# A gated attention trunk on one core: half of the memory's keys computed first, its norm applied after the product

## The reference

```
def rms_norm(x, g):
    y = x * rsqrt(mean(x * x, axis=-1, keepdims=True) + EPS)
    return y * g
...
memn = rms_norm(mem, norm_mem[l])           # 256 x 1024
h = h + cross_attention(hn, memn, w_xq[l], w_xkv[l], w_xo[l])
...
def cross_attention(hn, memn, wq, wkv, wo):
    q = (hn @ wq).reshape(B, S, X_HEADS, X_HD)
    k, v = jnp.split(memn @ wkv, 2, axis=-1)
    logits = einsum('bqhd,bkhd->bhqk', q, k) * (X_HD ** -0.5)
    p = softmax(logits)
    return einsum('bhqk,bkhd->bqhd', p, v).reshape(B, S, D_MODEL) @ wo
```

## Time and profile before

| | |
|---|---|
| median of 3 runs | 958.43 us (957.01 to 958.47) |
| profiled execution | 958.45 us |
| its span on the core | 956.7 us |
| TensorE, matmuls busy | 938.0 us |
| VectorE busy | 551.8 us |
| ScalarE busy | 408.9 us |
| GpSimd busy | 14.6 us |
| HBM read, written | 89.76 MB, 2.10 MB |
| DMA, mean | 97 GB/s |
| mean granted TensorE clock | 0.997 |

### The profile page before, as it was taken

The page is one execution under the profiler, slowest core; times in us unless marked ns, Lnnn a source line. Parts: engine busy times, 40 slices in busy tenths (PEclk is TensorE's granted clock), DMA queues, the critical chain, the costliest instruction groups (busy, mean ns, idle before and its releaser), DMA issues.

```text
span 956.7 us, 11786 instructions
## 1 busy us (share of the span) xinstructions
PE 938.0 (98%) x4605; PEld 762.0 (80%) x4605; DVE 551.8 (58%) x979; ACT 408.9 (43%) x676; POOL 14.6 (2%) x38
## 2 busy tenths in 40 slices
PE   7999999999998999999999999999999999999997
PEld 6878777777776878889988668888888888888885
DVE  6532676342547662778333534858947876885544
ACT  4431466444423323344434533455445545634522
POOL 4000000000000000000000000000000000000000
PEclk9999999999999999999999999999999999999999
DMA  8311221122112162442521242120441261063202
GB/s 288 128 42 53 89 88 45 45 88 88 48 41 89 45 228 83 140 143 77 211 88 36 97 175 78 55 89 1 151 158 45 87 221 45 1 202 107 88 1 88
DMA packets 44815, 92.62 MB, mean 97 GB/s; under 512 B 1772, under 2 KB 1864, under 8 KB 44760
## 3 DMA queue, kind: packets, MB, share of 16 engines
q1 hardware_dynamic: 43192, 86.54, 27.0%
q0 software_dynamic: 1568, 5.32, 1.7%
HBM read 89.76 MB, written 2.10 MB: 96 GB/s over the span
## 4 chain that ended last, share of the span: by engine, by line
PE 92%; DVE 4%; ACT 2%; issue 1%; DMA 1%; SPq 0%; ACTq 0%; DVEq 0%
PE bank L1341 68%; PE bank L1372 12%; PE bank L1545 1%; DVE w_lo L978 1%; PE bank L1439 1%; PE bank L1466 1%; PE bank L1451 1%; PE bank L1385 1%; PE bank L1496 1%; PE bank L1483 1%; PE bank L1523 1%; DMA stage<-in_w_in 1%; PE bank L1510 1%; ACT w_hi L727 1%; PE bank L1484 0%
## 5 line engine op out<-in xcount | busy, mean ns | idle before, releaser
L978 DVE TENSOR_TENSOR w_lo<-stage,w_hi 128x1024 fp32r<-128x1024 f32 x174 | 205.1, 1220 | 88.4 <-ACT w_hi L727 88.3
L1341 PE MATMUL bank<-act_hi,w_hi 128*128 128x512 f32 (+2 forms) x624 | 246.2, 394 | 1.1 <-DVE act_lo L1166 1.1
L1341 PE MATMUL bank<-act_hi,w_lo 128*128 128x512 f32 (+2 forms) x624 | 241.3, 387 | 0.0
L1341 PE MATMUL bank<-act_lo,w_hi 128*128 128x512 f32 (+2 forms) x624 | 240.8, 386 | 0.0
L727 ACT ACTIVATE w_hi<-stage 128x1024 fp32r<-128x1024 f32 x174 | 174.5, 1051 | 97.2 <-PE bank L1341 36.6
L1341 PEld LDWEIGHTS bank<-act_hi,w_hi 128*128 128x128 f32 x624 | 117.9, 189 | 23.4 <-issue 1.3
L1341 PEld LDWEIGHTS bank<-act_hi,w_lo 128*128 128x128 f32 x624 | 117.5, 188 | 23.9
L1341 PEld LDWEIGHTS bank<-act_lo,w_hi 128*128 128x128 f32 x624 | 117.8, 189 | 22.1
L1341 PE MATMUL bank<-w_hi,act_hi 128*128 128x512 f32 x256 | 101.6, 397 | 4.0 <-DVE act_lo L1166 2.6
L1341 PE MATMUL bank<-w_hi,act_lo 128*128 128x512 f32 x256 | 99.8, 390 | 0.0
L1341 PE MATMUL bank<-w_lo,act_hi 128*128 128x512 f32 x256 | 99.7, 390 | 0.0
(11 more groups left out here) (260 smaller groups left out, 1264.7 us busy)
## 6 DMA issues: line engine op xcount, KB each, us to landing
stage<-in_w_in SPq DMA_DIRECT2D x20, 1024.0 KB, 5.0
stage<-in_w_mlp_in SPq DMA_DIRECT2D x16, 1024.0 KB, 5.2
stage<-in_w_mlp_out SPq DMA_DIRECT2D x16, 1024.0 KB, 5.5
stage<-in_w_xkv SPq DMA_DIRECT2D x8, 1024.0 KB, 5.0
stage<-in_w_mix_out SPq DMA_DIRECT2D x4, 1024.0 KB, 4.9
stage<-in_w_xq SPq DMA_DIRECT2D x4, 1024.0 KB, 5.2
stage<-in_w_xo SPq DMA_DIRECT2D x4, 1024.0 KB, 5.0
x_tok<-in_x SPq DMA_DIRECT2D x4, 512.0 KB, 9.7
```

Source lines behind the costliest of these rows:

```text
L978: dve.tensor_tensor(w_lo[:, r:r + 2, :], stage_pair(pair), w_hi[:, r:r + 2, :].bitcast(F32), ALU.subtract).then_inc(s_low, 1)
L1341: ins = pe.matmul(dst, still[q], moving[q], start=(k == 0 and q == 0), stop=(k == nk - 1 and q == 2))
```

## The change

The unit mem_k0 is moved from after mix1 to the very front, ahead of fox_v, and is computed in another loop order: step k does all four groups with slab k, 12 matmuls of 256 columns, into banks 6 and 7 (`mem_products`). Its input is mem times the gains, without the roots: mem is loaded in two column halves, transposed (`mem_turn`), and split with the gain as a factor of the copy (`mem_split`), 256 columns at a time. The roots come later: squares on ScalarE, `mem_root` on VectorE, two diagonal tiles whose product with ones gives the factor of every memory row in all partitions (`mem_factors`), and the keys are multiplied by it as they leave PSUM (`mem_keys`, VectorE). The other half of the keys, mem_k1, stays in its place and is now taken out by VectorE with that factor instead of ScalarE's copy; the values get the root as the scale of their copy on ScalarE.

The split mem and the first keys are needed again after mix1, but their memory is not free in between. GpSimd writes them to DRAM (1 MB, 1 MB and 0.5 MB) and reads them back after the last merge_split. The zero padding of `conv_u` is written after those copies; ScalarE's conv and gate_rows steps and VectorE's fox_q wait for it (`s_pad`).

At the start the warm-up is 12 products (24 instructions), the load order is mem, gains, slab 0, slab 1, mem's other half, slabs 2-3, slabs 4-5, x tile 0, slabs 6-7, the row of norm_mix, fox_v's first lot, x tile 1, fox_v's second lot, x tiles 2 and 3. The norm steps of x are moved as the list shows: norm_turn of tiles 2 and 3 now stand after the second half of the group before, not after its first half.

```diff
-WARM_UP = 20
+WARM_UP = 12
...
     u = [
+        ("mem_k0", "w_xkv", 0, KT, 0, 4),
         ("fox_v", "w_in", 0, KT, C_FV, NT),
...
-        ("mem_k0", "w_xkv", 0, KT, 0, 4),
         ("mem_k1", "w_xkv", 0, KT, HALF_W, 4),
...
-    steps += [("norm", 0), ("split_weights", 0), ("norm_turn", 0), ("norm_split", 0), ("split_weights", 1),
-              ("norm", 1), ("split_weights", 2), ("norm_root", 1), ("split_weights", 3), ("norm_scale", 1)]
-    after(1, ("norm_turn", 1), ("norm_split", 1), ("norm", 2))
-    after(2, ("norm_turn", 2), ("norm_split", 2), ("norm", 3))
-    after(4, ("norm_turn", 3), ("norm_split", 3), ("split_weights", 4), ("split_weights", 5))
+    steps += [("mem_gains", 0), ("mem_turn", 0), ("mem_split", 0), ("split_weights", 0), ("mem_split", 1),
+              ("mem_turn", 1), ("mem_split", 2), ("mem_split", 3)]
+    after(0, ("split_weights", 1), ("mem_turn", 2), ("mem_split", 4), ("mem_split", 5))
+    after(1, ("split_weights", 2), ("mem_turn", 3), ("mem_split", 6), ("mem_split", 7))
+    after(2, ("split_weights", 3), ("norm", 0))
+    before(3, ("mem_squares", 0), ("mem_squares", 1))
+    after(3, ("split_weights", 4), ("split_weights", 5))
+    before(7, ("norm_turn", 0), ("norm_split", 0), ("norm", 1))
+    after(7, ("norm_root", 1), ("norm_scale", 1))
+    after(first("fox_v"), ("mem_root", 0))
+    after(first("fox_v") + 1, ("norm_turn", 1), ("norm_split", 1), ("norm", 2))
+    after(first("fox_v") + 2, ("mem_factors", 0), ("mem_keys", 0))
+    after(first("fox_v") + 3, ("norm_turn", 2), ("norm_split", 2), ("norm", 3))
+    after(first("fox_v") + 5, ("norm_turn", 3), ("norm_split", 3))
...
-    h = first("mix0")
-    for i in range(MEM // P):
-        after(h + 2 * i + 2, ("norm", NT + i))
-        after(h + 2 * i + 4, ("norm_turn", NT + i), ("norm_split", NT + i))
...
-        pairs.setdefault(f if early else max(f, min(f + 1, need - 2)), []).append(pair)
+        at_half = f if early else max(f, min(f + 1, need - 2))
+        pairs.setdefault(max(at_half, FIRST_HALF[1] - 1), []).append(pair)
...
+            pool.wait_ge(s_memhigh, KT)
+            pool.dma_start(kept_hi, mem_hi[:].bitcast(F32)).then_inc(s_kept, 16)
+            pool.wait_ge(s_memlow, KT)
+            pool.dma_start(kept_lo, mem_lo[:].bitcast(F32)).then_inc(s_kept, 16)
+            pool.wait_ge(s_memkeys, 4)
+            pool.dma_start(kept_k, mem_k[:, 0:4, :]).then_inc(s_kept, 16)
+            pool.wait_ge(s_kept, 16 * 3)
+            pool.memset(conv_u[:, :, 0:CONV_K - 1], 0.0).then_inc(s_pad, 1)
...
-            load_row(row_a, norm_mem, s_row_a)
-
-            pool.wait_ge(s_scaled, 2 * (NT + 2))
+            pool.wait_ge(s_merl, KT)
             load_row(row_b, norm_xattn, s_row_b)
+            pool.dma_start(mem_hi[:].bitcast(F32), kept_hi).then_inc(s_back, 16)
+            pool.dma_start(mem_lo[:].bitcast(F32), kept_lo).then_inc(s_back, 16)
+            pool.dma_start(mem_k[:, 0:4, :], kept_k).then_inc(s_back, 16)
...
-                elif k == "mem_k":
-                    copy(mem_k[:, 4 * order(n) + j, :], b[:, 0:MEM]).then_inc(free, 1)
...
-                    copy(mem_v[:, j, HALF_W * order(n):HALF_W * (order(n) + 1)], b[:]).then_inc(free, 1)
+                    copy(mem_v[:, j, HALF_W * order(n):HALF_W * (order(n) + 1)], b[:], scale=mem_stat[:, 2, j:j + 1])\
+                        .then_inc(free, 1)
...
+                elif step == "mem_split":
+                    act.wait_ge(s_memturn, n // 2 + 1)
+                    if n == 0:
+                        act.wait_ge(s_gain, 1)
+                    copy(mem_hi[:, n, :], mem_turned(n), scale=mem_gain[:, n:n + 1]).then_inc(s_memhigh, 1)
...
+                elif k == "mem_k":
+                    group_done(dve, g)
+                    dve.tensor_tensor(mem_k[:, 4 + j, :], b[:, 0:MEM], mem_factor[:], ALU.mult).then_inc(free, 1)
...
+                elif step == "mem_root":
+                    dve.wait_ge(s_memsquares, MEM // P)
+                    half_mean_square(mem_stat[:, 1, :], mem_stat[:, 0, :], DM)
+                    inverse_root(mem_stat[:, 2, :], mem_stat[:, 1, :], mem_stat[:, 3, :])
+                    for i in range(MEM // P):
+                        dve.tensor_scalar(mem_diag[:, i, :], ident[:], mem_stat[:, 2, i:i + 1], None, ALU.mult)\
+                           .then_inc(s_memdiag, 1)
+                elif step == "mem_keys":
+                    dve.wait_ge(s_half, KT)
+                    dve.wait_ge(s_memfactor, 1)
+                    for j in range(4):
+                        dve.tensor_tensor(mem_k[:, j, :], mem_product(j), mem_factor[:], ALU.mult).then_inc(s_memkeys, 1)
...
+            def mem_products(k):
+
+                pe.wait_ge(s_memlow, k + 1)
+                if k == 0:
+                    pe.wait_ge(s_slablow, 1)
+                elif k % 2 == 0 or k == 1:
+                    pe.wait_ge(s_low, k // 2 + 1)
+                for j in range(4):
+                    cols = slice(P * j, P * j + P)
+                    for q, (s, a) in enumerate(((w_hi, mem_hi), (w_hi, mem_lo), (w_lo, mem_hi))):
+                        ins = pe.matmul(mem_product(j), s[:, k, cols], a[:, k, :], start=(k == 0 and q == 0 and j % 2 == 0),
+                                        stop=(k == KT - 1 and q == 2 and j % 2 == 1))
+                ins.then_inc(s_half, 1)
```

More of the change, by code:

```diff
@@ L99 @@
 SLAB0 = [sum(u[3] for u in UNITS[:n]) for n in range(len(UNITS) + 1)]
-GROUP0 = [sum(u[5] for u in UNITS[:n] if u[3] <= KT) for n in range(len(UNITS) + 1)]
+GROUP0 = [sum(u[5] for u in UNITS[1:n] if u[3] <= KT) for n in range(len(UNITS) + 1)]
 def make_halves():
@@ L120, in make_halves @@
             groups = groups[2:]
+        if n == 0:
+            halves += [(n, j, c, 0, MEM) for c in cs for j in groups]
+            continue
         width = MEM if u[0].startswith("mem_k") else TOK
@@ L275, in make_steps @@
         after(first("up_ml1") + m - 4, ("merge_split", m))
-    h = first("mix0")
-    for i in range(MEM // P):
-        after(h + 2 * i + 2, ("norm", NT + i))
-        after(h + 2 * i + 4, ("norm_turn", NT + i), ("norm_split", NT + i))
-    for unit, n0, last in (("mix1", NT + 2, 5), ("x_out1", 2 * NT + 2, 3)):
+    for unit, n0, last in (("mix1", NT, 5), ("x_out1", 2 * NT, 3)):
         n = UNIT[unit]
@@ L657, in _ @@
             fill(pool.memset(ident[:], 0.0))
+            pool.wait_ge(s_const, n)
+            fill(pool.affine_select(out=ident[:], in_=ident[:], compare_op=ALU.not_equal, fill=1.0, base=0,
+                                    pattern=[[-1, P]], channel_multiplier=1))
+            assert n == N_IDENT
             fill(pool.memset(ident_b[:], 0.0))
@@ L664, in _ @@
             fill(pool.memset(decay[:].bitcast(F32), 0.0))
-            fill(pool.memset(conv_u[:], 0.0))
             fill(pool.memset(enter[:], 0.0))
@@ L668, in _ @@
             pool.wait_ge(s_const, n)
[L669 to L671 removed]
+            fill(pool.affine_select(out=ident_b[:], in_=ident_b[:], compare_op=ALU.not_equal, fill=1.0, base=0,
+                                    pattern=[[-1, P]], channel_multiplier=1))
             fill(pool.affine_select(out=hide_b[:], in_=hide_b[:], compare_op=ALU.is_ge, fill=HIDE, base=0,
@@ L1311, in source_ready @@
                 elif k % 4 == 0:
-                    tiles = {"mem_k": NT + 2, "mem_v": NT + 2, "x_q": 2 * NT + 2, "mlp_in": n_norm}.get(name, NT)
+                    if name in ("mem_k", "mem_v"):
+                        pe.wait_ge(s_back, 16 * 3)
+                        return
+                    tiles = {"x_q": 2 * NT, "mlp_in": n_norm}.get(name, NT)
                     if name == "mlp_in" and end < TOK:
@@ L1343, in half, with mem_turn @@
                 ins.then_inc(s_half, 1)
+            def mem_products(k):
[10 more added lines that the diff above has]
+                ins.then_inc(s_half, 1)
+            def mem_turn(b):
+                if b == 0:
+                    pe.wait_ge(s_const, N_IDENT)
+                pe.wait_ge(s_mem[b // 2], 16)
+                if b >= 2:
+                    pe.wait_ge(s_memlow, 2 * (b - 1))
+                for k in (2 * b, 2 * b + 1):
+                    for i in range(MEM // P):
+                        ins = pe.transpose(mem_turned(k)[:, P * i:P * i + P], mem_tok[:, i, P * k:P * k + P], ident[:])
+                ins.then_inc(s_memturn, 1)
             def product(i):
@@ L1555, in _ @@
                 if step == "half":
-                    product(n) if in_products(HALVES[n][0]) else half(n)
+                    if HALVES[n][0] == 0:
+                        mem_products(n)
+                    elif in_products(HALVES[n][0]):
+                        product(n)
+                    else:
+                        half(n)
+                elif step == "mem_gains":
+                    pe.wait_ge(s_const, N_IDENT)
+                    pe.wait_ge(s_gains, 16)
+                    pe.transpose(bank[1][:, 0:KT], gain_rows[:], ident[0:KT, 0:KT]).then_inc(s_gainturn, 1)
```

(8 more changed lines are left out.)

160 lines of the change are left out of this document (103 added, 57 removed).

## The result

The changed kernel took 975.14 us (median, 972.66 to 975.26) beside 958.45 for the kernel before (957.01 to 958.69): a ratio of 1.0172, interval 1.0157 to 1.0186. The forecast was 967, slower. The sign came, with nearly twice the size: +16.7 us where +9.0 stood in the sum, outside the range of 960.5 to 971.5. Its profiled execution took 975.26, its span 973.1.

The account below looks back on a forecast made before the run. The prediction took TensorE, busy 938.0 of 956.7 us, to bound the kernel. Start +4.8, clock +1.7 and middle +2.5 summed to +9.0 on 958.45, so 967 us, range 960.5 to 971.5.

Parts of the forecast that it names:

- the yardstick: At the start: fox_v has to end before 52.8 us, or the start has lost time.
- VectorE's queue: At the start: work ahead of tile 1's act_lo delays it to 34.1, so TensorE waits 5.4 us.
- the middle: At mem_k1: its copy, moved to VectorE behind two w_lo, makes TensorE wait 2.5 us (2.1 to 2.8).
- The floor: At the start: without the copies' delay fox_v ends at 54.6, +1.8 us; with loads that cost nothing 53.5, +0.7.
- the clock: Behind the wait for tile 1: granted clock falls to half, adding 1.7 us (0 to 3.4).
- the walk: Step-by-step timing of the start along the queues: fox_v ends at 54.6 before the copies to DRAM are added.
- Rival 2: At the start: 3.8 us earlier products are kept if tile 1's act_lo precedes 29 us; 957.3 or 954.8; 9%.
- the term for the loads: At the start: copies to DRAM delay later loads by up to 5.2 us; fox_v's end moves from +1.8 to +4.8.
- The start: Up to fox_v's end: +4.8 us taken, between ends of +1.8 and +7.1.
- Rival 3: At the start: too little warm-up, clock doesn't rise, memory unit at twice the pitch, fox_v ends at 63.4; 973; 8%.
- Rival 1: At the start: copies stay out of the loads' way and the clock holds; 961.7 to 962.8; 20%.
- Rival 4: After the start: waits for DRAM or the pad memset reach TensorE; 3% together with other ways.

Follow-up runs that it names:

- both late: Changed kernel with the copies to DRAM and the six small-element loads issued only after tile 1's lo part: 967.38 us, ratio 1.0105.
- the best kernel: Changed kernel with copies and small loads late, VectorE's mem_root, factors and fox_q splits later, tiles 2-3 turned earlier, x_q0's first splits later: 956.16 us, 0.9978.

## Why the prediction was right and wrong

**Right: the yardstick and VectorE's queue.** The 52.8 us at which fox_v has to end is the point where the time turns: 52.9 with VectorE's order mended, whose only other loss is the 2.3 us of the middle, gave 961.8; 50.0 gave 956.2. The order of VectorE's work was read right from the step lists, and its prices were right: tile 1's group at 34.58 for 34.1 once the loads were away, mem_root 2.2 us in both. The floor was too low all the same. Without either load fox_v ended 4.9 us behind the yardstick, 1.6 of it the clock, so 3.2 where the walk had 1.8 (and +0.7 for loads that cost nothing).

Rival 2 had the right lever and too much hope. It asked for tile 1's act_lo before 29 us, by pairs 8 and 9 and mem_root put later, and gave 957.3, or 954.8 with the middle mended. Those two moves, with the loads late, brought it to 30.71 and the time to 961.8. Only with tiles 2 and 3 turned earlier and the middle mended as well, and that act_lo at 29.82, did the kernel take 956.2.

**Right: the middle.** 2.3 us for 2.5 taken, by exactly the chain that was named: copy behind the two w_lo. VectorE and TensorE of the changed kernel:

```profile
475.10 2.35 DVE L1044 TENSOR_TENSOR w_lo<-stage,w_hi 128x1024 fp32r<-128x1024 f32 x2
...
477.37 0.75 DVE L1155 TENSOR_TENSOR mem_k<-bank,mem_factor 128x256 f32<-128x256 f32 x2
```
```profile
477.84 0.39 PE L1431 MATMUL bank<-mem_hi,w_hi 128*128 128x256 f32 x1 [2.27 <-DVE mem_k L1155]
```

**Wrong: the term for the loads.** The start was taken at +4.8, of which 3.0 were the loads (5.3 at full contention), and the clock was put at 1.7 beside it: +6.5. 13.0 came. The loads are 8.1 of it, the difference between the changed kernel (65.8) and the one with both late (57.65), at the same 1.6 of clock in each. The rest is the 3.2 above. Three steps failed.

1. Slabs 6-7 were put at 12.4, ahead of the sag. They are split at 14.1 with both loads late, and at 18.10 in the changed kernel: now they lie in the sag, which is as long as before (175 GB/s from 13 to 17 us, 189 in the kernel before). In the best kernel the small loads cost 3.9 us.
2. Copies were priced as a delay by their own bytes, 5.2 us, of which half was taken. From 20 to 25 us they held 75% of the engines, and q1 fell to 0.53 MB, where it moves 1.95 MB with the copies late. The lot that was in flight paid nearly all of it. The Trainium skill's page "DMA: Bandwidth & Descriptors", section "Queues, rings and completion order", which was cited for turns packet by packet, pointed at the right end, +7.1. The trace agrees that both queues are served at once; it doesn't decide on turns of one recorded packet, as the two kernels with smaller ones show.
3. The delay was charged to fox_v's second lot and what follows it; the walk named none for the first lot. It was the first lot that paid. It is split at 26.87 in the changed kernel and at 18.42 with both late, 8.4 us apart, and VectorE's queue behind it takes 15 us to tile 1's group in either (27.96 to 42.77, 19.52 to 34.58), so that nearly all of it, 8.2 us, reached tile 1. The two causes don't add: the first lot comes 2.6 us late with the small loads alone in their place (21.01), 2.0 with the copies alone (20.39, but then the second lot is late), and 8.4 with both. 3.9 and 0.6 were what taking away each alone showed of the 7.8.

**Right in size, partly by luck: the clock.** The fall behind the long wait came as forecast, and the start pays 1.6 us for it where 1.7 was taken. But there were two falls, behind two waits, and the longer one (6.8 us, from 30.1, a length that was not in the trace of before) cost TensorE 2.8 us that the wait for tile 1 hid. With VectorE's order mended and the loads left late it no longer hides, and the gain is 3.1 us instead of 5.6. With fox_v at the yardstick there is no fall in the start.

**Not seen: the fall at 333.9 us.** It stands behind a wait of 1.84 us for ml_den. The same wait is in the kernel before, without a fall; its line in the list of waits there:

```profile
PE bank L1483 <- DVE ml_den L1238: 2.5, 2, 1.8
```

TensorE of the changed kernel:

```profile
332.12 1.12 PE L1601 MATMUL bank<-ml_k,ml_q 128*128 128x512 f32 x2 [1.84 <-DVE ml_den L1325]
...
334.70 0.63 PE L1431 MATMUL bank<-act_lo,w_hi 128*128 128x512 f32 x1
335.13 0.63 PE L1431 MATMUL bank<-act_hi,w_lo 128*128 128x512 f32 x1
```

Matmuls 0.43 us apart instead of 0.23. It cost 1.6 of the 16.4 us. All seventeen profiled kernels have this wait, and three have the fall behind it: the changed one, the best kernel with its small loads early (at 324.0), and the kernel before with its small loads late (at 307.8). So it doesn't belong to the change; that it depends on where the work before it falls is a guess.

**Small or right.** The warm-up's 24 instructions took 5.4 us instead of 3.9, and the first memory product came at 9.1, not 7.1. In the changed kernel no cost of it is to be seen, since the products wait 1.7 us for slabs 6-7 in any case, until 20.56; where the loads are away it is not free, as the two kernels with the longer warm-up show. Rival 3, the cold start, did not come: the memory unit ran at full clock, and that its 973 is near the result is luck. Rival 1 was what the loads would have had to do; they did the opposite. Rival 4 didn't come.

## What to carry to other kernels

A copy to DRAM that nobody waits for is not free while the same engines bring what is wanted next: on another queue it can take most of them (70 to 82% here), so hold it back until the loads that the next wait hangs on have landed. On an in-order engine, list what stands ahead of each operation that the bounding engine waits for, and put splits and roots that are wanted later behind it; then a unit moved forward keeps its gain (956.16 here, for 975.14 with the same parts in another order). Two causes of one lateness have to be taken away together before either is judged, and a long wait of TensorE is to be priced with a possible stretch of half clock behind it (1.6 us for each 3.4 here), unless the next wait hides it.

## What the runs showed of the hardware that was not expected

- From 20 to 25 us the copies on GpSimd's queue held 70 to 82% of the DMA engines against loads on SP's queue with 20 to 32%: 72 to 82% with packets of 7 to 8 KB, 70 and 71% with 3.9 KB.
- Loads with tiny elements, beside large ones, held the 16 engines at a share of 0.99 with 175 GB/s for 4 us (201 at 0.92 with the copies late), where 367 pass without them. In the kernel before, the rate went from 189 to 401 without them, and the time didn't move (1.0001).
- The same wait of TensorE doesn't always bring the same fall of the granted clock. It stood at 0.50 for 6.8 us behind waits of 4.8 and 5.4 us, but for 3.4 us behind one of 5.0; for 3.4 us behind one of 2.4; and behind the 1.8 us wait for ml_den in three profiled executions of seventeen.
- 24 warm-up instructions took 4.3 to 5.5 us from one kernel to another, with the same code.
